# Conformer centring and variance as products of rounded parts, its last step behind a split

## The reference

```python
def group_norm_channels(x, g, b):
    bsz, s, c = x.shape
    xf = x.astype(jnp.float32).reshape(bsz, s, CONF_GROUPS, c // CONF_GROUPS)
    mu = jnp.mean(xf, axis=-1, keepdims=True)
    var = jnp.mean(jnp.square(xf - mu), axis=-1, keepdims=True)
    y = ((xf - mu) * lax.rsqrt(var + GN_EPS)).reshape(bsz, s, c)
    return (y * g.astype(jnp.float32) + b.astype(jnp.float32)).astype(x.dtype)

def conformer_conv_mixer(u, dw_w, dw_b, gn_g, gn_b):
    val, gate = jnp.split(u, 2, axis=-1)
    z = val * jax.nn.sigmoid(gate)
    z = causal_depthwise_conv(z, dw_w) + dw_b        # 31 taps
    z = group_norm_channels(z, gn_g, gn_b)           # 4 groups of 64 channels
    return jax.nn.silu(z)
```

## Time and profile before

| | |
|---|---|
| median of three runs | 1293.1 us |
| profiled execution, its own time | 1293.34 us |
| its span, first to last instruction | 1291.6 us |
| TensorE busy | 1283.1 us, 99% |
| VectorE busy | 736.3 us, 57% |
| ScalarE busy | 563.4 us, 44% |
| granted clock of TensorE | 1.00 (2.4 GHz) |
| HBM read | 128.07 MB, 101 GB/s over the span |

### The profile page before, as it was taken

One profiled execution on the slowest core, in us unless ns is written; L12 is line 12 of the kernel. 1 busy time (PEld: TensorE's weight loads), 2 busy tenths in 40 slices (PEclk: granted clock), 3 DMA queues, 4 the chain that ended last, 5 costly groups with the idle time before them and its releaser, 6 DMA issues.

```text
span 1291.6 us, 16219 instructions
## 1 busy us (share of the span) xinstructions
PE 1283.1 (99%) x6558; PEld 1076.4 (83%) x6558; DVE 736.3 (57%) x1085; ACT 563.4 (44%) x958; POOL 7.0 (1%) x8
## 2 busy tenths in 40 slices
PE   9999999999999999999999999999999999999998
PEld 9877898898889888888888898777898888888886
DVE  5757678576587555555533579776663433433333
ACT  4577644235425444444522355575443422322221
POOL 0000001000000000000000000000000000000000
PEclk9999999999999999999999999999999999999999
DMA  7322244312234333333433143123143333333311
GB/s 257 135 82 66 99 131 145 149 50 82 82 92 129 106 98 99 98 98 98 147 98 98 33 136 110 54 66 114 49 148 98 98 98 98 115 98 98 98 49 65
DMA packets 38002, 131.22 MB, mean 102 GB/s; under 512 B 4356, under 2 KB 5636, under 8 KB 37672
## 3 DMA queue, kind: packets, MB, share of 16 engines
q1 hardware_dynamic: 37928, 130.19, 32.3%
HBM read 128.07 MB, written 2.10 MB: 101 GB/s over the span
## 4 chain that ended last, share of the span: by engine, by line
PE 98%; DVE 1%; ACT 0%; DMA 0%; issue 0%; SPq 0%; DVEq 0%; ACTq 0%
PE bank L1233 18%; PE bank L1234 17%; PE bank L1235 17%; PE bank L1346 5%; PE bank L1348 5%; PE bank L1351 5%; PE bank L1347 5%; PE bank L1349 5%; PE bank L1350 5%; PE bank L1411 1%; PE bank L1277 1%; PE bank L1288 1%; PE bank L1488 1%; PE bank L1474 1%; PE bank L1282 1%; PE bank L1433 1%
## 5 line engine op out<-in xcount | busy, mean ns | idle before, releaser
L1233 PE MATMUL bank<-xh,whi 128*128 128x512 f32 (+1 forms) x1168 | 421.8, 361 | 0.1
L1234 PE MATMUL bank<-xl,whi 128*128 128x512 f32 (+1 forms) x1168 | 415.8, 356 | 0.0
L1235 PE MATMUL bank<-xh,wlo 128*128 128x512 f32 (+1 forms) x1168 | 415.6, 356 | 0.0
L2061 DVE TENSOR_TENSOR wlo<-stage,whi 128x1024 fp32r<-128x1024 f32 (+1 forms) x222 | 267.5, 1210 | 229.8 <-ACT whi L1606 229.6
L1606 ACT CAST whi<-stage 128x1024 fp32r<-128x1024 f32 (+1 forms) x222 | 228.9, 1036 | 199.6 <-PE bank L1351 157.2
L1233 PEld LDWEIGHTS bank<-xh,whi 128*128 128x128 f32 x1168 | 220.7, 189 | 38.6 <-issue 7.5
L1235 PEld LDWEIGHTS bank<-xh,wlo 128*128 128x128 f32 x1168 | 220.7, 189 | 31.8
L1234 PEld LDWEIGHTS bank<-xl,whi 128*128 128x128 f32 x1168 | 220.8, 189 | 30.7 <-issue 0.7
L1346 PE MATMUL bank<-whi,xh 128*128 128x512 f32 x281 | 110.5, 393 | 0.6 <-DVE wlo L2061 0.4
L1347 PE MATMUL bank<-whi,xh 128*128 128x512 f32 x281 | 109.4, 389 | 0.0
L1348 PE MATMUL bank<-wlo,xh 128*128 128x512 f32 x281 | 109.4, 389 | 0.0
(11 more groups left out here) (334 smaller groups left out, 1381.2 us busy)
## 6 DMA issues: line engine op xcount, KB each, us to landing
stage<-in_W_m SPq DMA_DIRECT2D x64, 512.0 KB, 3.6
stage<-in_W_up SPq DMA_DIRECT2D x44, 512.0 KB, 3.6
stage<-in_W_down SPq DMA_DIRECT2D x22, 512.0 KB, 3.6
stage<-in_W_in_a SPq DMA_DIRECT2D x19, 512.0 KB, 3.9
stage<-in_W_out SPq DMA_DIRECT2D x16, 512.0 KB, 3.7
stage<-in_W_in_b SPq DMA_DIRECT2D x10, 512.0 KB, 3.6
stage<-in_W_kv_k SPq DMA_DIRECT2D x8, 512.0 KB, 3.7
stage<-in_W_kv_v SPq DMA_DIRECT2D x8, 512.0 KB, 3.8
```

The lines of the kernel that those rows point to most:

```text
L1233: e.matmul(b[:, cols], hi[:, k, :], xh[:, k, cols], start=(k == 0), stop=False)
L1234: e.matmul(b[:, cols], hi[:, k, :], xl[:, k, cols], start=False, stop=False)
L1235: last = e.matmul(b[:, cols], lo[:, k, :], xh[:, k, cols], start=False, stop=(k == 7))
L2061: e.tensor_tensor(wlo[:, plan.place[i], c], stage[:, i % NSTAGE, c], whi[:, plan.place[i], c].bitcast(F32), ALU.subtract).then_inc(S["w_lo"])
```

## The change

- The plain products of `cf_mean` and `cf_var` become two products each: the constant matrix, copied once into a rounded form (`cen_r`, `bo_r`, in the half of `first` that is free then), by the high part and by the low part of `cy[q]`, or of `cq[q]`.
- A new step `cf_parts(q)` makes the parts of `cy[q]`: a cast on ScalarE, a subtraction on VectorE. It stands ahead of `lru_b`. The parts of the squares are made in `cf_mean(q)` on both engines. They lie in a weight slot that `keep("cf")` takes before `cf_parts` and `give` returns after `cf_var`, so that five slots are left in between.
- `tap(60)`, which takes all taps still to be issued, stands ahead of `cf_parts` and not behind `lru_b`; no taps are left at either place.
- ScalarE's part of `cf_scale` is a step of its own, `cf_gate`, two stages later, where `cf_out` was. `cf_out` stands behind the split of the output's tile 1.
- The cast of `first` for out2 waits for the second variance product as well, which reads `bo_r` there.

```diff
@@ Plan
     def cf_mean(self):
         for q in range(2):
             self.fill("cf_mean", q)
             self.step("cf_mean", q)
             self.out(("cf_mean", q), "cf_s", q + 1)
+            self.x_split("cf_square", q)
...
         tap(4)
         yield
+        tap(60)
+        self.keep("cf")
+        for q in range(2):
+            self.step("cf_parts", q)
+            self.x_split("cf_parts", q)
         self.step("lru_b")
-        tap(60)
         yield
...
         self.cf_var()
+        self.give("cf", "cf_v_full", 2)
         self.cf_scale()
         self.step("first", "out2")
         yield
         for q in range(2):
-            self.step("cf_out", q)
+            self.step("cf_gate", q)
...
             if q:
                 self.step("x_from", "out2", 1)
                 self.x_split("out2", 1)
+                for c in range(2):
+                    self.step("cf_out", c)
             self.step("sc_b", q)
@@ tensor
             def cf_mean(c):
                 b = fill("cf_mean", c)
-                q.wait_ge(S["ld_mix2"], 64)
-                q.wait_ge(S["cf_taps"], c + 1)
-                e.matmul(b[:], cen, cy[c], start=True, stop=True).then_inc(S["cf_m_full"])
+                q.wait_ge(S["x_lo"], plan.x_at["cf_parts", c])
+                e.matmul(b[:], cen_r, cf_hi[:, c, :], start=True, stop=False)
+                e.matmul(b[:], cen_r, cf_lo[:, c, :], start=False, stop=True).then_inc(S["cf_m_full"])
 
             def cf_var(c):
                 b = fill("cf_var", c)
-                q.wait_ge(S["cf_sq"], c + 1)
-                e.matmul(b[:], bo, cq[c], start=True, stop=True).then_inc(S["cf_v_full"])
+                q.wait_ge(S["x_lo"], plan.x_at["cf_square", c])
+                e.matmul(b[:], bo_r, cf_hi[:, c, :], start=True, stop=False)
+                e.matmul(b[:], bo_r, cf_lo[:, c, :], start=False, stop=True).then_inc(S["cf_v_full"])
@@ scalar
+            def cf_parts(c):
+
+                if c == 0:
+                    q.wait_ge(S["ld_mix2"], 64)
+                    q.wait_ge(S["mm"], CHUNK0["down"] + 1)
+                    e.copy(cen_r, cen)
+                    e.copy(bo_r, bo)
+                    q.wait_ge(S[plan.kept["cf"][1][0]], plan.kept["cf"][1][1])
+                q.wait_ge(S["cf_taps"], c + 1)
+                e.copy(cf_hi[:, c, :], cy[c]).then_inc(S["x_hi"])
+
             def cf_mean(c):
                 q.wait_ge(S["cf_m_full"], c + 1)
                 e.activation(cq[c], bank_of("cf_mean", c)[:], ACT.Square).then_inc(S["cf_sq"])
+                q.wait_ge(S["cf_sq"], c + 1)
+                e.copy(cf_hi[:, c, :], cq[c]).then_inc(S["x_hi"])
@@ vector
+            def cf_parts(c):
+                q.wait_ge(S["cf_taps"], c + 1)
+                q.wait_ge(S["x_hi"], plan.x_at["cf_parts", c])
+                e.tensor_tensor(cf_lo[:, c, :], cy[c], cf_hi[:, c, :].bitcast(F32), ALU.subtract).then_inc(S["x_lo"])
+
+            def cf_mean(c):
+                q.wait_ge(S["cf_sq"], c + 1)
+                q.wait_ge(S["x_hi"], plan.x_at["cf_square", c])
+                e.tensor_tensor(cf_lo[:, c, :], cq[c], cf_hi[:, c, :].bitcast(F32), ALU.subtract).then_inc(S["x_lo"])
```

More of the change, by code:

```diff
@@ L536, in x_of @@
     def x_of(self, name):
-        return {"in_a": self.x_at["x", 7], "xq": self.x_at.get(("out1", "turn", 3, 1))}.get(name, self.x)
+        return {"in_a": self.x_at["x", 7], "xq": self.x_at.get(("out1", "turn", 3, 1)),
+                "in2_b": self.x_at.get(("down", "turn", 3, 1))}.get(name, self.x)
     def feat_mid(self, name, n, mid):
@@ L1154, in build_program @@
         cen = reg(64, 128, 3260 + 4614)
+        cf_hi, cf_lo = (tiles(w[:, plan.kept["cf"][0], :], 2) for w in (whi, wlo))
+        cen_r, bo_r = first[:, 1, 0:128], first[:, 1, 128:256]
         cg = par[:, NPAR + 16:NPAR + 20]
@@ L1657, in first_in @@
                     q.wait_ge(S["lru_h"], 1)
+                    q.wait_ge(S["cf_v_full"], 2)
                 e.copy(first[:, 0, :], source_of(name, 0)).then_inc(S["f_hi"])
@@ L1904, in cf_exp, with cf_gate @@
                     e.activation(cq[c], cq[c], ACT.Exp, scale=-0.5).then_inc(S["cf_ex"])
-            def cf_scale(c):
+            def cf_gate(c):
                 q.wait_ge(S["cf_s"], c + 1)
@@ L2037, in _ @@
                         warm=warm, layer_norm=layer_norm, xq=xq, xa_k=xa_k, xa_v=xa_v, xa_exp=xa_exp, xa_turn=xa_turn, decay=decay,
-                        xa_pv=xa_pv, up=up, rms_stats=rms_stats, rms_late=rms_late, ln_apply=ln_apply, last_norm=last_norm, cf_in=cf_in, cf_first=cf_first, cf_mean=cf_mean,
-                        cf_var=cf_var, cf_exp=cf_exp, cf_scale=cf_scale, in2_a=in2_a, in2_v=in2_v,
+                        xa_pv=xa_pv, up=up, rms_stats=rms_stats, rms_late=rms_late, ln_apply=ln_apply, last_norm=last_norm, cf_in=cf_in, cf_first=cf_first, cf_parts=cf_parts, cf_mean=cf_mean,
+                        cf_var=cf_var, cf_exp=cf_exp, cf_gate=cf_gate, in2_a=in2_a, in2_v=in2_v,
                         mb_score=mb_score, mb_norm=mb_norm, mb_turn=mb_turn, lru_in=lru_in, lru_gate=lru_gate,
@@ L2608, in _ @@
                         rms_apply=rms_apply, rms_late=rms_late, gain=gain, ln_sums=ln_sums, ln_apply=ln_apply,
-                        last_norm=last_norm, cf_in=cf_in, cf_tap=cf_tap, cf_scale=cf_scale,
+                        last_norm=last_norm, cf_in=cf_in, cf_tap=cf_tap, cf_parts=cf_parts, cf_mean=cf_mean, cf_scale=cf_scale,
                         cf_out=cf_out, mb_score=mb_score, mb_norm=mb_norm, mb_pv=mb_pv, lru_in=lru_in, lru_a=lru_a,
```

## The result

| | before | after |
|---|---|---|
| median, 22 runs each | 1294.07 us | 1291.35 us |
| lowest and highest | 1293.06 to 1295.97 | 1290.47 to 1293.06 |
| profiled execution, own time | 1293.34 us | 1291.04 us |
| span | 1291.6 us | 1289.2 us |
| TensorE busy | 1283.1 us | 1280.7 us |

The ratio of after to before is 0.998, 95% interval 0.9975 to 0.9986: 2.7 us less in the medians, where 2.8 was forecast. The forecast of 1290.3 started from 1293.1, the median of the first three runs of before; over 22 runs that median is 1294.07, 0.97 higher, and the measured 1291.35 lies 1.05 above the forecast.

A forecast was written before the change was run, and what follows sets the result against it. TensorE, busy for 99% of the span, was taken as the bound. Products 1.65 plus holes 1.15 gave 2.80 us, from the median of 1293.1 to 1290.3 us; range 1290.0 to 1291.6.

The forecast's parts named there:

- the holes stay: Rival: TensorE's two waits near 891 and 893 us stay in part or whole, 1290.6 to 1291.5 us; chance 0.34.
- both terms as counted: The case where products save 1.65 us and closed holes 1.15; chance 0.54, of which 0.48 under 1290.5.
- Products, 1.65: Centring and variance on TensorE: four f32 products, 3.46 us, become eight of rounded parts, 1.81; saves 1.65 us.
- the 0.05 for the spacing behind plain products: Slower spacing of some 0.23 us right behind the f32 pairs may go too, saving some 0.05 us more.
- Holes, 1.15: TensorE's waits for VectorE at out2's third tile and the next tile's k = 1 product close; saves 1.15 us.
- Two moves, one reason: Moving `cf_out` behind the split takes 1.21 us from VectorE's queue ahead of both holes; `cf_gate`'s move costs nothing.
- The margin of 0.3: VectorE's low part at the second split is seen at 890.37 us, TensorE asks at 890.69: margin 0.3 us.
- New waits and slots, nothing: TensorE's waits for the new parts have margins of 0.7 to 2 us; five weight slots instead of six cost nothing.
- The small casts: ScalarE's two new casts of 128 columns: at most 0.37 us each, taken as 0.2.
- Table loads, slower: Rival: ScalarE changes tables around every cast, 1.28 us each, 6.1 lost against 2.8 gained, 1296.4 us; chance 0.04.

The follow-up runs named there:

- e1: The changed kernel with `cf_gate` and `cf_out` back in their old places, so only the products change; 1.0025 of the kernel before, 1297.44 against 1294.81 us.
- e6: The changed kernel with the variance as plain f32 products again, the centring still in parts; 0.9987 of the kernel before, 1291.56 against 1293.66 us.
- e2: The kernel before with only the moves of `cf_gate` and `cf_out`, plain f32 products kept; 0.9996 of the kernel before, 1294.07 against 1294.81 us.
- e3: The changed kernel with only the gate activations back ahead of the cast of `first`; 1.0012 of the kernel before, 1296.31 against 1294.81 us.
- e9: The kernel of e1 profiled a second time; 35.99 us from the first centring product to the late tile's first product, one run.
- e10: The kernel of e1 profiled a third time; 35.98 us from the first centring product to the late tile's first product, one run.
- e4: The changed kernel with two unused VectorE sums of 128x512 added ahead of `sc_b(0)`; 0.9987 of the kernel before, 1292.47 against 1294.81 us.
- e7: The changed kernel with a second weight slot held back, leaving four; 0.9978 of the kernel before, 1290.59 against 1293.66 us.
- e8: The kernel of e3 profiled once more; 34.80 us from the first centring product to the late tile's first product, one run.

## Why the prediction was right

The saving was forecast as 2.80 and is 2.72 in the medians, 2.87 in the stretch, and both terms of the sum are there. That the time itself, 1291.35, still lies within the stated 1290.0 to 1291.6 is in part luck: the upper end had been set for a case in which the holes stay, and it also took up the 0.97 by which the three runs of before had been low. The chance of 0.48, with both terms as counted, for a time under 1290.5 rested on those three runs as well and did not come true.

- *Products, 1.65.* This was right. Eight starts took 1.82 us, against 3.46 (the changed kernel and e1 agree, and e6 for the four of the centring), and the 0.05 for the spacing behind plain products came out near 0.07: 2.87 - 1.65 - 1.15. With four passes (the Trainium skill, FP8 and Floating Point Precision, TensorE Precision Notes) at an ordinary start each, an estimate, the term would have been 1.81. The trace does not agree with that price, 0.86 us against 0.91 (e6); the number of passes stays open.
- *Holes, 1.15.* This was right in size, and its arithmetic held to 0.02 us over 16 us of VectorE's queue. e2 shows the same 1.16 without the products.
- *Two moves, one reason.* Here the working was too short. It put the closing of the holes down to `cf_out`, 1.21 us, and said of `cf_gate` only that it does no harm. In e3 `cf_out` is where the change has it and the hole is 2.69. The place of the gate activations behind the cast of `first` is worth 2.9 us of VectorE's queue at the low part of `first` and 3.3 at `sc_b(0)`, and is the larger of the two. The count used it silently, since it let `first`'s low part follow `cf_scale` at once. Neither move was run alone on the kernel before, so their shares with the plain products in place are not shown.
- *The terms are not independent.* The sum 1.65 + 1.15 reads as if each could be had alone. The moves can (e2); the products alone cost: 3.9 + 0.4 of holes against 1.15 before (e1), and in e9 and e10 half a clock behind them. The rival "the holes stay", 1290.6 to 1291.5, priced them at no more than before; had the order not been changed, it would have been 1294.6 by the stretch of e1 (1293.1 + 1.47), or 1295.8 with the half clock of e9 (1293.1 + 2.74).
- *The margin of 0.3.* It is 0.28 by the trace, and real: e4, with 1.33 us more in the queue, opened both holes.
- *New waits and slots, nothing.* This was right: there is no bracket at the four products, and e7 takes a further slot at no cost. The small casts took 0.30 with steps of 0.20, the value taken.
- *Table loads, slower.* This rival fell: between 871.64 and 873.32 squares and casts follow each other on ScalarE without a load, as at 869.05 before.

What the forecast took too lightly is the measurement. Three runs within 0.06 us looked like the whole spread; 22 runs spread over 2.9 us for before and 2.6 for after. In the twelve profiles the centring starts between 867.94 and 870.47, and most of that is there at the first transposes of TensorE, between 36.5 and 38.8 us, some 800 us ahead of anything the change touches. What moves them there is not shown.

## What to carry to other kernels

Where one engine is the bound, count the other engines' queues forward to each point at which they are asked, with the bounding engine's own shift: the margins of 0.65 and 0.28 us here said more than the busy shares. An edit that saves on the bounding engine but adds to a helper's queue is to be tried together with the reordering that pays for it, since alone it can lose. And ask of every step in a helper's queue that waits on another engine what stands behind it: four activations in front of one cast were worth more than two multiplications taken out.

## What the hardware showed that I had not expected

- A hole of 2.7 or 3.9 us in TensorE's work was followed in four of five profiles (e3, e8, e9, e10) by some 3.4 us at a granted clock of 0.50 (1.2 GHz), starts 0.43 us apart. The starts there lost 1.7 us; the stretch grew by some 1.3, since a hole of 0.28 behind it closed. The holes of 0.68 and 0.67 us (before, e4) had no such effect.
- In the fifth profile (e1), the same kernel as e9 and e10 with a hole of the same length, the clock stayed at 1.00. What decides between the two is not shown.
- After each hole, however short, the first start is followed by a step of 0.30 or 0.31 us in place of 0.23.
